# Two feed-forward networks: the down projection of hidden chunks 0 to 15 in seven half-size products, laid between gate-and-up units

## The reference, cut to what matters

```
def swiglu(x, w_gu, w_down):
    g, u = jnp.split(x @ w_gu, 2, axis=-1)
    return (jax.nn.silu(g) * u) @ w_down
...
h = h + swiglu(rms_norm(h, ffn_norm[layer]), ffn_w_gu[layer], ffn_w_down[layer])
```

## Time and profile before

| | us |
|---|---|
| median of three runs | 2185.53 |
| span of the profiled execution, first to last instruction | 2183.0 |
| TensorE busy | 2151.1 (99%) |
| VectorE busy | 1359.8 (62%) |
| ScalarE busy | 1023.8 (47%) |
| first network, seven-product stretches | 509.4 to 572.2 and 638 to 738 |
| first network, down projection | 572.2 to 638 and 738 to 793 |

### The profile page before, as it was taken

The page is one execution under the profiler, slowest core; times in us unless marked ns, Lnnn a source line. Parts: engine busy times, 40 slices in busy tenths (PEclk is TensorE's granted clock), DMA queues, the critical chain, the costliest instruction groups (busy, mean ns, idle before and its releaser), DMA issues.

```text
span 2183.0 us, 31617 instructions
## 1 busy us (share of the span) xinstructions
PE 2151.1 (99%) x12122; PEld 1818.0 (83%) x12122; DVE 1359.8 (62%) x2066; ACT 1023.8 (47%) x1552; POOL 320.9 (15%) x267
## 2 busy tenths in 40 slices
PE   8999999999999999999999999999999999999998
PEld 6788887789989988877889899878778878888887
DVE  6766667379759733555697498366676655555522
ACT  5445555345325434565444254365566544444312
POOL 0221212220000120003200000300111143222211
PEclk9999999999999999999999999999999999999999
DMA  3311111122323322201223223321221222222221
GB/s 142 116 59 39 59 39 39 59 97 78 118 79 113 117 97 78 97 20 41 95 78 136 77 97 131 139 97 40 73 73 39 84 105 97 96 96 96 97 97 58
DMA packets 31666, 184.89 MB, mean 85 GB/s; under 512 B 3104, under 2 KB 7712, under 8 KB 11312
## 3 DMA queue, kind: packets, MB, share of 16 engines
q1 hardware_dynamic: 29520, 175.48, 22.7%
q0 software_dynamic: 2016, 7.60, 1.1%
HBM read 178.84 MB, written 7.37 MB: 85 GB/s over the span
## 4 chain that ended last, share of the span: by engine, by line
PE 93%; DVE 3%; ACT 3%; issue 1%; DMA 0%; SPq 0%; POOL 0%; DVEq 0%; POOLq 0%; ACTq 0%
PE ps L2334 26%; PE ps L2336 25%; PE ps L2335 25%; PE ps L2658 2%; PE ps L3149 1%; PE ps L3092 1%; PE ps L3132 1%; PE ps L2652 1%; PE ps L3159 1%; PE ps L2924 1%; PE ps L2964 1%; PE ps L2682 1%; DVE sq L2008 0%; ACT wh L514 0%; DMA raw<-in_stream 0%
## 5 line engine op out<-in xcount | busy, mean ns | idle before, releaser
L2334 PE MATMUL ps<-xh,wh 128*128 128x512 f32 (+1 forms) x1584 | 603.6, 381 | 4.0 <-POOL xl L2284 2.1
L2336 PE MATMUL ps<-xh,wl 128*128 128x512 f32 (+1 forms) x1584 | 578.2, 365 | 0.0
L2335 PE MATMUL ps<-xl,wh 128*128 128x512 f32 (+1 forms) x1584 | 576.8, 364 | 0.0
L1228 DVE TENSOR_TENSOR wl<-raw,wh 128x2048 fp32r<-128x2048 f32 x104 | 241.4, 2321 | 231.4 <-ACT wh L514 231.2
L2334 PEld LDWEIGHTS ps<-xh,wh 128*128 128x128 f32 x1584 | 299.4, 189 | 54.6 <-issue 12.7
L2336 PEld LDWEIGHTS ps<-xh,wl 128*128 128x128 f32 x1584 | 298.4, 188 | 49.3
L2335 PEld LDWEIGHTS ps<-xl,wh 128*128 128x128 f32 x1584 | 299.3, 189 | 43.7 <-issue 4.3
L514 ACT ACTIVATE wh<-raw 128x2048 fp32r<-128x2048 f32 x104 | 198.8, 1912 | 233.5 <-PE ps L2336 233.2
L2336 PE MATMUL ps<-part_h,wl 128*128 128x512 f32 x512 | 201.7, 394 | 0.0
L2335 PE MATMUL ps<-part_l,wh 128*128 128x512 f32 x512 | 200.6, 392 | 0.0
L2334 PE MATMUL ps<-part_h,wh 128*128 128x512 f32 x512 | 199.7, 390 | 0.0
(11 more groups left out here) (419 smaller groups left out, 3916.0 us busy)
## 6 DMA issues: line engine op xcount, KB each, us to landing
raw<-in_stream SPq DMA_DIRECT2D x158, 1024.0 KB, 4.8
hankd<-tabd SPq DMA_DIRECT2D x1, 3072.0 KB, 16.9
hank<-hankd POOLq DMA_DIRECT2D x4, 768.0 KB, 5.1
hT<-in_xT SPq DMA_DIRECT2D x4, 512.0 KB, 6.7
keepd<-hT POOLq DMA_DIRECT2D x1, 2048.0 KB, 10.1
hT<-keepd POOLq DMA_DIRECT2D x8, 256.0 KB, 5.4
out<-hT SPq DMA_DIRECT2D x8, 256.0 KB, 2.5
raw<-in_stream SPq DMA_DIRECT2D x2, 512.0 KB, 8.5
```

Source lines behind the costliest of these rows:

```text
L1228: dve.tensor_tensor(wl[:, s, :], raw[:, s, :], wh[:, s, :].bitcast(F32), ALU.subtract).then_inc(lo_made, 1)
L2334: pe.matmul(out, w_hi, a_hi, start=start, stop=False)
L2335: pe.matmul(out, w_hi, a_lo, start=False, stop=False)
L2336: return pe.matmul(out, w_lo, a_hi, start=False, stop=stop)
```

## The change

- Six plain gate-and-up units instead of five and one in four pieces. Behind them one stream of 24 seven-product units: gates 6 to 9, four down units (hidden chunks 0 to 7), gates 10 to 17, four down units (chunks 8 to 15), gates 18 to 21. Then three plain down units over chunks 16 to 21.
- A down unit covers two output chunks and eight hidden chunks. Its products are added straight into hT (`add_half`), seven adds of 256 columns.
- The hidden chunks are taken by twos: four token sums (`pair_sums`), the high halves on ScalarE (`pair_hi`), the low ones on VectorE (`pair_lo`), written beside the other steps of a piece.
- Sums of products are left to PSUM: pieces 2, 3 and 6 add to the bank of piece 0, piece 5 to that of 4. Between them VectorE or ScalarE reads what stands there: three copies on ScalarE and three adds on VectorE per gate unit, in place of one copy and six adds. A piece waits until the sum it adds to is read (`taken`). Six banks are used as two sets of three, one per unit in turn.
- The order of a unit's pieces is 2, 1, 4, 3, 0 of the next, 5, 6 (it was 1, 2, 3, 4, 0 of the next, 5, 6). The weight sums are made one piece ahead of the low half (`sums`), the first two together.
- Silu is taken over 512 columns at once; hidden chunks wait in a ring of four.
- The weight stream on the host is laid in that order.

```
-PLAIN, CUT = 5, 12
+PLAIN, PARTS = 6, 12
...
-GROUPS = ((PLAIN, CUT, "PSSSSSS", (12, 13, 22, 23, 32, 33)), (CUT, FC, "SSSSSSSSSS", (30, 31)))
...
+HALVES = ((10, 0), (18, 4))
+REST = 16
+LEAD = 4
+SETS = ((4, 5, 0), (1, 2, 3))
+BANK_OF = {0: 0, 2: 0, 3: 0, 6: 0, 1: 1, 4: 2, 5: 2}
+QUARTER_OF = {0: (0, 0), 1: (0, 0), 2: (0, 1), 5: (0, 1), 4: (1, 1), 3: (1, 1), 6: (1, 0)}
...
+    units = []
+    for n in range(PLAIN, FC):
+        for at, first in HALVES:
+            if n == at:
+                units += [("down", i) for i in range(first, first + 4)]
+        units.append(("gate", n))
+    return units
...
+def pieces():
+
+    order = [(0, 0)]
+    for j in range(len(STREAM)):
+        order += [(j, 2), (j, 1), (j, 4), (j, 3)]
+        if j + 1 < len(STREAM):
+            order.append((j + 1, 0))
+        order += [(j, 5), (j, 6)]
     return order
...
+PAIR_SUMS_AT = {1: 1, 5: 2, DONE_AT[DOWN_AT[3]] + 1: 4}
+PAIR_SUMS_AT.update({DONE_AT[GATE_AT[2 * m + 1]] + 3: m for m in (3, 5, 6, 7)})
+HIDDEN_AT = {DONE_AT[DOWN_AT[7]] + 1: REST, DONE_AT[DOWN_AT[7]] + 2: REST + 1}
+HIDDEN_AT.update({DONE_AT[GATE_AT[n]] + 3: n for n in range(REST + 2, FC)})
...
+        def result_of(j, k):
+            return ps[:, SETS[j % 2][BANK_OF[k]], 0:TOK]
...
+        def taken(f, j, k):
+            kind, n = STREAM[j]
+            if kind == "down":
+                return half_added, fast_count(half_added, f, ADDS[j, k])
+            if k == 6:
                 return prod_made, FC * f + n + 1
-            return added(f, n, min(k, 5))
+            return join_made(f, j, k) if k == 3 else fork_made(f, j, k)
...
+                def pair_hi(m):
+                    i = m % 4
+                    act.wait_ge(pair_summed, fast_count(pair_summed, f, 4 * m + 4))
...
+                    act.activation(xh[:, i, TOK:], act_of(2 * m)[:, 0:TOK], ACT.Copy)
+                    act.activation(part_h[:, 3 * i, :], act_of(2 * m + 1), ACT.Copy)
+                    act.activation(part_h[:, 3 * i + 1, :], ssq[:, :], ACT.Copy).then_inc(hid_hi_made, 1)
+                    act.activation(part_h[:, 3 * i + 2, :], sq[:, :], ACT.Copy).then_inc(hid_hi_made, 1)
...
+                def products():
+                    for p in range(len(ORDER) + 4):
+                        if p + LEAD < len(ORDER):
+                            hi(*ORDER[p + LEAD])
+                        elif p < len(ORDER):
+                            down_hi(p + LEAD - len(ORDER))
+                        j, k = ORDER[p - 1] if 0 < p <= len(ORDER) else (None, None)
+                        if j in GATES and k in (0, 2, 4):
+                            copy_out(j, k)
+                        j, k = ORDER[p - 2] if 1 < p <= len(ORDER) + 1 else (None, None)
+                        if j in GATES and k == 5:
+                            act.wait_ge(*join_made(f, j, 5))
+                            silu(STREAM[j][1])
+                        if p - 1 in PAIR_SUMS_AT:
+                            pair_hi(PAIR_SUMS_AT[p - 1])
+                        if p in HIDDEN_AT:
...
+                            hidden(HIDDEN_AT[p])
 
                 split_hi(u0 + 1)
...
+                def gated(j):
...
+                    left, right = act_of(n)[:, 0:TOK], act_of(n)[:, TOK:]
+                    dve.tensor_tensor(left, left, result_of(j, 6), ALU.mult)
+                    dve.tensor_tensor(right, right, scaled[:, 1, TOK:], ALU.mult).then_inc(prod_made, 1)
...
+                def pair_sums(m):
+                    dve.wait_ge(prod_made, FC * f + 2 * m + 2)
...
+                    a, b, n = act_of(2 * m), act_of(2 * m + 1), 4 * m
+                    b11, b12, b21, b22 = a[:, 0:TOK], a[:, TOK:], b[:, 0:TOK], b[:, TOK:]
+                    dve.tensor_tensor(ssq[:, 0:TOK], b12, b11, ALU.subtract).then_inc(pair_summed, 1)
+                    dve.tensor_tensor(sq[:, 0:TOK], b22, b12, ALU.subtract).then_inc(pair_summed, 1)
+                    dve.wait_ge(pair_summed, fast_count(pair_summed, f, n + 1))
+                    dve.tensor_tensor(ssq[:, TOK:], b22, ssq[:, 0:TOK], ALU.subtract).then_inc(pair_summed, 1)
+                    dve.wait_ge(pair_summed, fast_count(pair_summed, f, n + 3))
...
+                    dve.tensor_tensor(sq[:, TOK:], b21, ssq[:, TOK:], ALU.subtract).then_inc(pair_summed, 1)
...
+                def pair_lo(m):
...
+                    dve.wait_ge(hid_hi_made, FC * f + 2 * m + 2)
+                    dve.tensor_tensor(xl[:, i, TOK:], act_of(2 * m)[:, 0:TOK], xh[:, i, TOK:].bitcast(F32), ALU.subtract)
+                    dve.tensor_tensor(part_l[:, 3 * i, :], act_of(2 * m + 1), part_h[:, 3 * i, :].bitcast(F32), ALU.subtract)
+                    dve.tensor_tensor(part_l[:, 3 * i + 1, :], ssq[:, :], part_h[:, 3 * i + 1, :].bitcast(F32), ALU.subtract).then_inc(hid_lo_made, 1)
+                    dve.tensor_tensor(part_l[:, 3 * i + 2, :], sq[:, :], part_h[:, 3 * i + 2, :].bitcast(F32), ALU.subtract).then_inc(hid_lo_made, 1)
...
+                def first_sums(j):
...
                     dve.tensor_tensor(wsum[:, 0, :], q[2], q[3], ALU.add).then_inc(weights_summed, 1)
...
+                    dve.wait_ge(weights_summed, fast_count(weights_summed, f, 4 * j + 1))
                     dve.tensor_tensor(wsum[:, 1, :], wsum[:, 0, :], q[0], ALU.subtract).then_inc(weights_summed, 1)
...
+                def difference(j):
...
+                    q = raw_quarters(j)
...
                     dve.tensor_tensor(q[2], q[0], q[2], ALU.subtract).then_inc(weights_summed, 1)
...
+                def last_sum(j):
+                    q = raw_quarters(j)
...
                     dve.tensor_tensor(q[1], q[1], wsum[:, 1, :], ALU.subtract).then_inc(weights_summed, 1)
...
+                def sums(j, k):
+                    if k == 2:
+                        first_sums(j)
+                    elif k == 3:
+                        difference(j)
+                    elif k == 5:
+                        last_sum(j)
...
+                def add_half(j, k):
...
+                    h = hT[:, 2 * (i % 4) + row, TOK * col:TOK * col + TOK]
+                    dve.tensor_tensor(h, h, result_of(j, k), ALU.add).then_inc(half_added, 1)
...
+                def products():
+                    for p in range(len(ORDER) + 5):
+                        if p + LEAD < len(ORDER):
+                            lo(*ORDER[p + LEAD])
+                        elif p < len(ORDER):
+                            down_lo(p + LEAD - len(ORDER))
+                        if p + LEAD + 1 < len(ORDER):
+                            sums(*ORDER[p + LEAD + 1])
+                        j, k = ORDER[p - 1] if 0 < p <= len(ORDER) else (None, None)
+                        if j not in GATES and j is not None:
+                            add_half(j, k)
+                        elif k == 1:
...
+                        j, k = ORDER[p - 2] if 1 < p <= len(ORDER) + 1 else (None, None)
+                        if j in GATES and k == 6:
+                            gated(j)
+                        if p in PAIR_SUMS_AT:
+                            pair_sums(PAIR_SUMS_AT[p])
+                        if p - 2 in PAIR_SUMS_AT:
+                            pair_lo(PAIR_SUMS_AT[p - 2])
+                        if p - 1 in HIDDEN_AT:
+                            hidden_lo(HIDDEN_AT[p - 1])
...
+                def down_operand(k, m):
+                    if k == 0:
+                        return xh[:, m, TOK:], xl[:, m, TOK:]
+                    part, side = {1: (0, 0), 5: (0, 1), 4: (1, 0), 2: (1, 1), 3: (2, 0), 6: (2, 1)}[k]
+                    tok = slice(TOK * side, TOK * side + TOK)
+                    return part_h[:, 3 * m + part, tok], part_l[:, 3 * m + part, tok]
...
-                        if k < 7:
-                            x_hi, x_lo = operand(k, i)
...
+    def ffn_fast(gu, down):
+        c, d = by_chunk(gu), by_chunk(down)
+        gates, first = np.stack([c[:FC], c[FC:]], 1), 0
+        for end, hidden in ((10, 0), (18, 8)):
+            add(gates[first:end])
+            add(d[:, [hidden + i for i in (0, 2, 4, 6, 1, 3, 5, 7)]])
+            first = end
+        add(gates[first:])
+        add(d[:, REST:])
+
+    ffn_fast(w["ffn_w_gu"][0], w["ffn_w_down"][0])
```

More of the change, by code:

```diff
@@ L131, in slots_of @@
[L131 to L147, removed]
@@ new lines, in pieces, with running @@
+def pieces():
[5 more added lines that the diff above has]
+        order += [(j, 5), (j, 6)]
+    return order
+def running(kept):
+    count, n = {}, 0
+    for p in ORDER:
+        n += kept(*p)
+        count[p] = n
+    return count
+STREAM = stream_units()
+ORDER = pieces()
+GATE_AT = {n: j for j, (kind, n) in enumerate(STREAM) if kind == "gate"}
+DOWN_AT = {i: j for j, (kind, i) in enumerate(STREAM) if kind == "down"}
@@ new lines @@
+GATES = set(GATE_AT.values())
+DONE_AT = [ORDER.index((j, 6)) for j in range(len(STREAM))]
+SPLITS = running(lambda j, k: k != 6)
+FORKS = running(lambda j, k: STREAM[j][0] == "gate" and k in (0, 2, 4))
```

(22 more changed lines are left out.)

537 lines of the change are left out of this document (202 added, 335 removed).

## The result

The changed kernel takes 2274.32 us (median of 4 runs, 2273.5 to 2275.2) against 2185.44 for the kernel before: ratio 1.041, 95% interval 1.039 to 1.042. The forecast was 2270, range 2228 to 2290.

A forecast was written before the change was run, and what follows sets the result against it. TensorE was taken to set the pace everywhere, with VectorE as full in the streams. In us, 2183.0 - 16.0 (TensorE's saving) + 98.0 (stream stalls) + 2.4 (rest) = 2267.4, plus 2.5 around the span: 2270, range 2228 to 2290.

The forecast's parts named there:

- TensorE's saving of 16.0 us: Down units over hidden chunks 0 to 15, 16 in both networks, each go from 10.99 to 9.99 us on TensorE.
- VectorE's cycle: VectorE's time per unit in the streams: 10.43 us for gate-and-up and down units alike, against TensorE's 9.99.
- all three trips of a unit: VectorE's sums for pieces 3, 5, 2 wait on ScalarE's high halves: 0.79 us each bare, 0.46 with an operation between.
- the rival in which half of them lie under other waits: In the streams half the round trips lie under waits for TensorE: 2222 us; chance 0.06.
- Pairs: In the stream, hidden chunks taken by twos mostly add 5.13 us each on VectorE, 2.0 of it waiting behind ScalarE's copies.
- The stream: Per network, 24 seven-product units paced by VectorE take 288.8 us against TensorE's 239.8, so TensorE stalls 49.0 us.
- the entry: VectorE enters the stream late, after the last plain unit: 3.3 us, of which pair work brings 0.8 (0 to 1.4).
- The rest: Behind the stream, VectorE's split and low halves delay the add that frees TensorE's bank: 1.2 us per network (0 to 2).
- the granted clock should stay: Expected sign after the change: TensorE's granted clock stays where it is, at 9 tenths in all forty profile slices.
- The rival's price (382 us): The granted clock falls in the stalls, so TensorE's pieces take 2.86 us in the streams: 2652 us; chance 0.02.
- pair copies that don't hold (2245): In the streams ScalarE's pair copies fall where VectorE has other work: 12.6 us per network go, 2245 us; chance 0.14.
- VectorE keeping pace (2169.5): VectorE's bare work of 232.4 us per stream fits in TensorE's 239.8, so the kernel gets faster: 2169.5 us; chance 0.10.

The follow-up runs named there:

- second experiment: Changed kernel with ScalarE's four copies per hidden pair put one to a step and VectorE's four low halves three and four steps later: 2250.25 us.
- the eighth: Changed kernel with sums, copies and low halves of hidden pairs 4 to 7 narrowed to 8 columns, leaving out most of that computation: 2240.22 us.
- seventh experiment: Kernel of the sixth experiment with VectorE's first residual add of each weight unit behind the stream made ahead of its 2048-column low half: 2203.46 us.
- fifth experiment: Changed kernel with weight sums two pieces ahead, pair copies one to a step, and the pair's sums and low halves spread evenly: 2201.11 us.
- sixth experiment: Kernel of the fifth experiment with the four sums of pairs 1 to 7 on GpSimd and ScalarE's copies one or two steps later: 2205.80 us.
- the fourth: Kernel before the change with three of a unit's four weight sums made directly ahead of the low half that reads them: 2250.58 us.
- the tenth: Kernel of the fifth experiment with residual adds first behind the stream and piece 0's copy-out and the fifth high half before silu at its head: 2196.68 us.

## Why the prediction was right

- TensorE's saving of 16.0 us can't be read by itself, since no unit runs at TensorE's pace. The streams, with 24 units at 9.99 taken off, fit it: 2183.0 - 16.0 + 51.2 + 51.6 + 3.7 = 2273.5 by its terms as measured, against a span of 2272.8.
- VectorE's cycle: down unit 10.44 (forecast 10.43), gate-and-up unit 10.64 (10.43). The missing 0.2 is a fourth wait: behind the trip of piece 2 the next low half starts after 0.80 and not 0.60, because ScalarE has a copy out of PSUM between the two high halves. So all three trips of a unit are felt, and the rival in which half of them lie under other waits is out. The price of 0.33 for an add into hT, which no row had, holds (596.69 to 597.02). So does the 0.12 for a sum that reads the one before it: 659.64 to 660.37 is 0.73 and not 0.60, so the dependent sums weren't free.
- Three trips per unit: shown twice, by taking them out (34 us less) and by putting them into the kernel before (66 more). The trips of both streams add up to 87 us (32 units at 2.04 and 16 at 1.38); only 34 come back when they alone go, since a quiet unit can fall no further than from 10.64 or 10.44 to TensorE's 9.99. (The rival with half of the trips took 24 x 1.0 per network; with the down units at 1.38 it is 22, and 2226 for its 2222.) 0.79 per bare trip was right to the hundredth. An add or join of 0.33 in between leaves 0.46.
- Pairs: 15.64 forecast as 10.43 + 5.13 = 15.56. The second experiment shows ScalarE's hold (24 us), the eighth the whole price.
- The stream: 290.95 and 291.36 us, forecast 288.8. Of the 2.2 too few in the first, 0.9 lie at the entry: VectorE's product for the last plain unit starts at 515.35, so with its 0.60 the entry takes 4.2 us from 511.74 and not 3.3. The pair work ahead of it brought 1.7 where the range ended at 1.4. The other 1.3 are of the size of the 0.2 in each of nine quiet gate-and-up units.
- The rest: 34.84 us where three units of the kernel before take 32.97, so 1.9 per network and not 1.2, inside its 0 to 2. The seventh experiment, which frees the bank earlier, takes 1.5 of it away.
- Entry, quiet unit and rest came out above the forecast by 0.9, 0.2 and 0.7. Below it came pair 4, whose two units take 25.3 (608.06 to 633.37) where 10.43 twice and 5.13 are 26.0. No large errors cancel in the 2270.
- Wrong: "the granted clock should stay". It fell in the streams (below). It cost little here: units within the streams in which it fell mostly keep VectorE's period, 15.64 with it and without. Two places show a price. From the first weight sum of the stream's first unit to that of its second the changed kernel takes 14.21 and 14.20 us, the eighth experiment with the same instructions there 13.58 and 13.59, and the clock is low for 6.8 us in the one and 3.4 in the other: 0.6 per network. One unit of the second stream with the low clock in it takes 12.58 where its twin in the first takes 12.12. That is 1.7 us of the 89. The rival's price (382 us) supposed a low clock all through.
- Among the rivals, pair copies that don't hold (2245) and VectorE keeping pace (2169.5) both needed another program. Built, they came to 2250 and 2197. The second is 27 us off, with most trips and holds gone. That lumps of pair work, which a lead of four pieces and the wait for the weights don't smooth, are the reason is likely from the fifth experiment (17 us from spreading them), but what is left after it stays open.

## What to carry to other kernels

Where two engines make an operand together (sum, high half, low half), the order of the instructions in the first one's queue decides, not its busy share: a value must be made at least one operation before the other engine's answer to it is wanted, or each trip costs 0.8 us in full. Work moved into a stage must be priced against the busiest engine's bare cycle there: here 8.29 us of a unit's 9.99 left room, the pairs filled it to 232.4 of 239.8, and the best order found left the change 0.6% slower than no change. Blocks of copies in the helping engine's queue need spreading, and a second engine on the same memory is no free help. TensorE's stalls can cost more than their length: at the head of the sixth experiment's streams 0.9 us more of stall went with the lower clock, and with 2.3 and 3.2 us more of time.

## What the runs showed of the hardware

TensorE's clock. In the windows of the changed kernel behind long stalls of TensorE (columns as in the earlier trace rows, the clock is the third from the end):

```profile
516.80:522.90 6.10, 6.10 (x29) 6.10 (x30) 3.48 (x8) 3.39 (x7) 0.00 (x0) 0.50 0.01 3
677.20:683.30 6.10, 6.08 (x28) 6.10 (x29) 5.40 (x10) 1.78 (x3) 0.00 (x0) 0.50 0.01 3
690.00:696.00 6.00, 6.00 (x53) 6.00 (x52) 4.60 (x10) 3.21 (x6) 0.00 (x0) 1.00 0.08 33
```

In the first two the granted clock is at its lower level of 1.2 GHz, and 29 products are made in the time of 53. The first follows a stall of 3.4 us, the second one of 2.8, and there are eleven such spells of 3.4 to 6.8 us in the two streams, 58 us of 582 in all. The fifth experiment and the fourth have none. That stalls bring them is what the place of the spells suggests; no run set out to test it. The length of the one stall ahead doesn't decide it: the stall of 2.79 us that ends at 650.94 is as long as that at 677.22, and behind it the clock stays at its upper level:

```profile
650.90:657.50 6.60, 5.92 (x48) 5.74 (x48) 5.47 (x10) 2.19 (x4) 0.00 (x0) 1.00 0.00 0
```

In the fifth experiment a stall of 2.53 us (to 516.03) brings no fall, in the tenth one of 2.00 (to 548.70) is followed by one.
